# Head norms of a 1-core transformer kernel: squares as two rounded parts, two fp32r products of ones in place of one fp32 product

## The reference

```python
def rms_norm(x, w):
    xf = x.astype(jnp.float32)
    y = xf * lax.rsqrt(jnp.mean(xf * xf, axis=-1, keepdims=True) + EPS)
    return (y * w.astype(jnp.float32)).astype(x.dtype)

# hgrn2_mixer, o: (B, S, heads, 128)
o = rms_norm(o, gate_norm_w) * jax.nn.silu(g...)
return o.reshape(B, S, D_MODEL) @ w_out
# diff_attn_mixer, o: (B, S, heads, 128)
o = rms_norm(o, subln_w) * (1.0 - lam_init)
return o.reshape(B, S, D_MODEL) @ w_out
```

## Time and profile before

| | us |
|---|---|
| median of 3 runs | 2556.8 (2556.59 to 2557.85) |
| the profiled execution's own time | 2557.45 |
| its span in the trace | 2554.4 |
| PE busy | 2499.1 (98% of the span) |
| DVE busy | 1471.3 (58%) |
| ACT busy | 1166.2 (46%) |
| POOL busy | 162.2 (6%) |

### The profile page before, as it was taken

The page is one execution under the profiler, slowest core; times in us unless marked ns, Lnnn a source line. Parts: engine busy times, 40 slices in busy tenths (PEclk is TensorE's granted clock), DMA queues, the critical chain, the costliest instruction groups (busy, mean ns, idle before and its releaser), DMA issues.

```text
span 2554.4 us, 34537 instructions
## 1 busy us (share of the span) xinstructions
PE 2499.1 (98%) x13736; PEld 2033.0 (80%) x13736; DVE 1471.3 (58%) x2374; ACT 1166.2 (46%) x2099; POOL 162.2 (6%) x156
## 2 busy tenths in 40 slices
PE   9999999999999999999989999999999999999998
PEld 6888778888776688888867888888877877788886
DVE  6665554433756565344378888786666556543343
ACT  5454352322456644233256666665455444432232
POOL 2110110000200020000101111111000010100001
PEclk9999999999999999999999999999999999999999
DMA  4222134534322223323232222222321233233322
GB/s 153 76 61 73 58 101 120 127 104 120 98 82 73 66 83 99 99 91 99 91 94 72 67 64 69 73 76 75 95 65 60 93 122 100 76 105 99 95 95 74
DMA packets 197088, 226.41 MB, mean 89 GB/s; under 512 B 7553, under 2 KB 132769, under 8 KB 196673
## 3 DMA queue, kind: packets, MB, share of 16 engines
q1 hardware_dynamic: 196928, 224.21, 29.6%
HBM read 214.22 MB, written 9.44 MB: 88 GB/s over the span
## 4 chain that ended last, share of the span: by engine, by line
PE 83%; DVE 9%; ACT 5%; issue 2%; DMA 0%; POOL 0%; DVEq 0%; SPq 0%; ACTq 0%; POOLq 0%
PE bank L1978 23%; PE bank L1980 22%; PE bank L1979 22%; PE bank L1984 2%; PE bank L1986 2%; PE bank L1985 2%; DVE CV L2710 1%; DVE wlo L2474 1%; PE bank L1997 1%; PE bank L2185 1%; PE bank L2161 1%; ACT whi L2253 1%; DVE h L2508 1%; PE bank L2193 1%; ACT XAh L2262 1%
## 5 line engine op out<-in xcount | busy, mean ns | idle before, releaser
L2474 DVE TENSOR_TENSOR wlo<-raw,whi 128x1024 fp32r<-128x1024 f32 x389 | 489.3, 1264 | 632.5 <-ACT whi L2253 630.3
L2253 ACT ACTIVATE whi<-raw 128x1024 fp32r<-128x1024 f32 x389 | 408.7, 1058 | 587.8 <-PE bank L1980 575.2
L1978 PE MATMUL bank<-XAh,whi 128*128 128x512 f32 x1552 | 616.4, 397 | 12.1 <-issue 5.2
L1980 PE MATMUL bank<-XAh,wlo 128*128 128x512 f32 x1552 | 602.6, 388 | 0.0
L1979 PE MATMUL bank<-XAl,whi 128*128 128x512 f32 x1552 | 602.5, 388 | 0.0
L1978 PEld LDWEIGHTS bank<-XAh,whi 128*128 128x128 f32 x1552 | 292.1, 188 | 91.2 <-issue 23.9
L1980 PEld LDWEIGHTS bank<-XAh,wlo 128*128 128x128 f32 x1552 | 292.1, 188 | 61.3
L1979 PEld LDWEIGHTS bank<-XAl,whi 128*128 128x128 f32 x1552 | 292.4, 188 | 57.5 <-issue 1.0
L1978 PE MATMUL bank<-XBh,whi 128*128 128x512 f32 (+1 forms) x840 | 331.2, 394 | 1.8 <-DVE XBl L2480 1.7
L1980 PE MATMUL bank<-XBh,wlo 128*128 128x512 f32 (+1 forms) x840 | 324.0, 386 | 0.0
L1979 PE MATMUL bank<-XBl,whi 128*128 128x512 f32 (+1 forms) x840 | 323.9, 386 | 0.0
(11 more groups left out here) (346 smaller groups left out, 3329.9 us busy)
## 6 DMA issues: line engine op xcount, KB each, us to landing
raw<-in_w_in SPq DMA_DIRECT2D x77, 512.0 KB, 3.8
raw<-in_up SPq DMA_DIRECT2D x64, 512.0 KB, 3.6
raw<-in_down SPq DMA_DIRECT2D x64, 512.0 KB, 3.7
raw<-in_a_w_in SPq DMA_DIRECT2D x32, 512.0 KB, 4.1
raw<-in_w_up SPq DMA_DIRECT2D x32, 512.0 KB, 3.7
raw<-in_w_down SPq DMA_DIRECT2D x32, 512.0 KB, 3.4
raw<-in_w_kv SPq DMA_DIRECT2D x16, 512.0 KB, 3.6
raw<-in_w_ssd_branch SPq DMA_DIRECT2D x16, 512.0 KB, 3.5
```

Source lines behind the costliest of these rows:

```text
L1978: pe.matmul(out, wh[:, w, c], xh[:, x, r], start=st, stop=False)
L1980: m = pe.matmul(out, wl[:, w, c], xh[:, x, r], start=False, stop=en)
L2253: act.activation(s.hi, s.raw, ACT.Copy).then_inc(s.whi[0], 1)
L2474: dve.tensor_tensor(s.lo, s.raw, s.hi.bitcast(F32), ALU.subtract).then_inc(s.wlo[0], 1)
```

## The change

For the 8 heads of the first mixer and the 8 of the attention, the step `sq` becomes `sq_parts`: ACT squares the bank in fp32 (`sq`), then squares it again with fp32r output (`sqp`, part 0); DVE subtracts part 0 from `sq` and writes the rest as fp32r (`sqp`, part 1). The step `ones` becomes `ones_parts`: two fp32r products of a rounded matrix of ones, one per part, into the same bank. The product waits for the subtraction. There is one buffer `sqp` in each stage; a head's generator waits for it (`his.room(1)`), where attention's heads had two buffers `sq` to wait for. The setup rounds the ones once on ACT and its semaphores are regrouped; `lwork` moves into the first stage's memory.

```diff
+    def square_parts(src, ready, his):
+        q, hi = sqs.take(), his.take()
+        e = add("sq_parts", src=src, src_ready=ready, q=q, hi=hi, sq=sig("sq"), hi_done=sig("sq"), lo_done=sig("sq.lo"))
+        q.free(e.lo_done)
+        return hi, e.lo_done
+
+    def parts_sum(hi, ready, bank):
+        s = add("ones_parts", hi=hi, ready=ready, bank=bank, ones=sig("ones"))
+        hi.free(s.ones)
+        return s.ones
...
-            sq, sqt = square(ob.t[:, :], s7.val)
+            while not his.room(1):
+                yield WAIT
+            hi, lo = square_parts(ob.t[:, :], s7.val, his)
...
-            s8 = add("ones", q=sq, sq=sqt, bank=b, n=S, first=True, final=True, ones=sig("ones"))
-            sq.free(s8.ones)
-            r, rt = rms_close(b, s8.ones, P)
+            r, rt = rms_close(b, parts_sum(hi, lo, b), P)
...
-            while not ring_all.room(2) or not sqs.room(1):
+            while not ring_all.room(2) or not sqs.room(1) or not his.room(1):
                 yield WAIT
...
+        elif k == "ones_parts":
+            on.wait_ge(*K.onesr_ready)
+            on.wait_ge(*s.ready)
+            on.room(s.bank)
+            pe.matmul(s.bank.t[:, :], K.onesr[:, :], s.hi.t[:, 0, :], start=True, stop=False)
+            pe.matmul(s.bank.t[:, :], K.onesr[:, :], s.hi.t[:, 1, :], start=False, stop=True).then_inc(s.ones[0], 1)
...
+        elif k == "sq_parts":
+            on.wait_ge(*s.src_ready)
+            on.room(s.q)
+            act.activation(s.q.t[:, :], s.src, ACT.Square).then_inc(s.sq[0], 1)
+            on.room(s.hi)
+            act.activation(s.hi.t[:, 0, :], s.src, ACT.Square).then_inc(s.hi_done[0], 1)
...
+            act.activation(K.onesr[:, :], K.ones, ACT.Copy).then_inc(s.onesr[0], 1)
...
+        elif k == "sq_parts":
+            on.wait_ge(*s.sq)
+            on.wait_ge(*s.hi_done)
+            dve.tensor_tensor(s.hi.t[:, 1, :], s.q.t[:, :], s.hi.t[:, 0, :].bitcast(F32), ALU.subtract).then_inc(s.lo_done[0], 1)
```

More of the change, by code:

```diff
@@ L304, in make_plan @@
     rrs = Ring([Slot(sb(f"rr{i}", [P, S])) for i in range(2)])
-    K.epst, K.lwork, K.ls2 = sb("epst", [P, 1]), sb("lwork", [P, 128]), sb("ls2", [P, 4])
+    K.onesr = sb("onesr", [P, P], F32R)
+    K.epst, K.ls2 = sb("epst", [P, 1]), sb("ls2", [P, 4])
     K.ident, K.U, K.L, K.ones = (cst[:, c:c + 128] for c in (C_IDENT, C_U, C_L, C_ONES))
@@ L701, in make_plan @@
         over, ring_h = {}, ring_all
+        his = Ring([Slot(sb("sqp", [P, 2, S], F32R, scope=sc))])
+        K.lwork = sb("lwork", [P, 128], scope=sc)
         SCt = Ring([Slot(sb(f"SCt{i}", [P, S], scope=sc)) for i in range(4)])
@@ L878, in make_plan @@
             if k == 5:
-                s = add("setup", lam=sig("lam"), lb=sig("lb"), eps=sig("eps"), lam1=sig("lam1"), lam2=sig("lam2"), lb1=sig("lb1"), lb2=sig("lb2"))
-                K.lam, K.lb, K.eps = s.lam, s.lb, s.eps
+                s = add("setup", eps=sig("setup.dve"), lam1=sig("setup.dve"), lb1=sig("setup.dve"), lam=sig("setup.dve"), lb=sig("setup.dve"),
+                        lam2=sig("setup.act"), onesr=sig("setup.act"), lb2=sig("setup.act"))
+                K.lam, K.lb, K.eps, K.onesr_ready = s.lam, s.lb, s.eps, s.onesr
             split(XB, k, hsrc(k), ht[k], scale=col(gain["a_norm_pre"] + k), src2=K.gain_in)
@@ L1217, in values @@
             hs[hd]["at"].free(s1.val)
-            q, sq = square(ob.t[:, :], s1.val)
+            hi, lo = square_parts(ob.t[:, :], s1.val, his)
             yield
@@ L1223, in values @@
             b = ring_all.take()
-            s3 = add("ones", q=q, sq=sq, bank=b, n=S, first=True, final=True, ones=sig("ones"))
-            q.free(s3.ones)
+            ones_done = parts_sum(hi, lo, b)
             add("act_table", name="natural_log_exp_and_others")
-            r, rt = rms_close(b, s3.ones, P)
+            r, rt = rms_close(b, ones_done, P)
             yield
```

## The result

The changed kernel takes 2561.98 us, the median of 19 runs (2560.45 to 2566.7); the kernel before, run beside it, 2556.95 (19 runs, 2555.97 to 2558.19). The ratio is 1.002, with a 95% interval of 1.0013 to 1.0027: 5.0 us slower. The forecast was 1.5 slower, so the loss is 3.5 us larger than forecast, and that needs an explanation. The time itself is 3.7 us above the stated 2558.3, at the very edge of the range.

A forecast was written before the change was run, and what follows sets the result against it. PE, busy 98% of the span, was taken to bound the kernel. First mixer -2.0, attention heads 0 to 3 +4.8, heads 4 to 7 -1.3 make +1.5 on the median 2556.8: 2558.3 us, range 2553.0 to 2562.0.

The forecast's parts named there:

- The freed 0.41 us a head, first mixer -2.0: First mixer: shorter products free 0.41 us at each of seven heads, last head 0.85 later; -2.0 in all.
- rival C: First mixer: DVE's shift reaches PE there too, four of seven heads lose; +5.6 beyond the forecast, 2563.9; chance 12%.
- Attention, heads 0 to 3, +4.8: Reciprocals wait in DVE's list behind the subtraction, PE starts later: 1.4 + 1.0 + 1.4 + 1.0 = +4.8 us.
- rival B: Middle heads of the attention: the waits are absorbed, -4.9 us in all, 2551.9; chance 13%.
- Attention, heads 4 to 7, -1.3: Four shorter products gain 1.6 and a vanished wait 0.6, head 4's wait costs 1.0; walked through in order -1.3 us.
- Head 4's wait: Attention head 4: PE reaches the product of ones before the subtraction is done and waits 1.0 us.
- the wait of 0.58 for rr: Attention, at 878.90: PE's wait for a bank that rr frees goes, as head 5's product leaves its way.
- From there the subtractions are ready before PE comes: Attention, after head 4: each value product has a whole piece, 2.7 us, behind it, so PE finds subtractions done.
- Rival D, the clock: Mixer's last head and later stages: one clock fall comes or goes, about 1.7 us either way, 2556.6 or 2560.0; chance 15%.
- the 3.2 of the prediction: Last head of the first mixer: PE idles 3.2 us in place of 2.35.
- its own +1.4 at head 0: Attention head 0: ACT's L2327 starts 1.4 us late behind the held reciprocals, and PE starts 1.4 later.
- Rival E: Products of ones get less short than taken, 0.24 us freed a head: +2 on 12 heads, 2560.3; chance 5%.

The follow-up runs named there:

- the half by itself: Changed kernel with the attention's eight heads back to one square and one fp32 product, new form in the first mixer only: 2554.87 us, before 2556.85.
- the three kernels above: Changed kernel, attention's heads with one square and no DVE operation: 2553.69 us; two squares, no DVE operation: 2555.63; one square and a DVE addition: 2557.92.
- the first four experiments: Changed kernel with new form in first mixer only, 2554.87 us; attention only, 2565.02; attention head 5 back to fp32, 2561.05; attention's subtractions on POOL, 2563.08.
- x4_later2: Changed kernel with the attention's second square and subtraction one round later, products of ones a round after that: 2565.11 us, before 2557.34.

## Why the prediction was off

- **The freed 0.41 us a head, first mixer -2.0:** right. 0.4 at each of seven heads, PE's wait at the last one 1.97 (1.95 forecast), and the half by itself measured -2.0. None of PE's waits is new in heads 0 to 6 (0.68 and 0.96 us before and after), so rival C is out.
- **Attention, heads 0 to 3, +4.8:** right in mechanism, and nearly in size: 4.4 in two traces. The split into second square and subtraction is shown by the three kernels above, and rival B (the waits are absorbed) is out. The queue order held: the reciprocals didn't pass the subtraction.
- **Attention, heads 4 to 7, -1.3:** this step failed. Head 4's wait (0.87, forecast 1.0) was right, and the wait of 0.58 for rr went. Wrong was "From there the subtractions are ready before PE comes": they were, but head 7's product waits 1.91 us for a bank instead. I had followed only what the product reads and not where it writes. The tail lost 0.7 where 1.3 were to be gained, which puts the sum 2.0 us off. The same 1.91 without any subtraction shows that the bank and the order make this wait. With the order of before back, the wait is 0.87 and the trace's loss in the tail is gone; the median gives 0.9 us back.
- **Rival D, the clock:** the other half. I gave one fall of 1.7 us 15%, at either sign, and placed it at the mixer's last head. It came there too, and cost nothing, because PE waited behind it anyway. (PE idles 1.97 + 1.65 = 3.6 us at that head without a fall, not the 3.2 of the prediction, which left out that the shorter product makes the wait longer.) Two more came, behind the waits that the change itself made or made longer, and cost 3.2 us in the profiled execution. The forecast left them out of its sum; one of them stood behind the wait that its own +1.4 at head 0 made longer.
- **Sum by the trace:** -2.2 + 4.4 + 0.7 + 3.2 - 0.4 = +5.7, against a span 5.6 longer. The median's loss is 3.5 above the forecast's. By the traces 2.0 of that is the tail; the rest I put down to the clock, but that is argued and not shown. A hint are the granted clocks of all timed runs: 0.9955 on average over the 19 of the changed kernel, 0.9970 over the 28 of before beside the first four experiments. A fall of 3.4 us takes 0.0007 of a run's average, so that is about two falls more in each run, an estimate, at most 1.7 us each. The -0.4 behind the attention I did not trace to a cause.
- Rival E, products less short, is out: 0.23 apart.

## What to carry to other kernels

When PE's wait behind a place names ACT or DVE, an operation put into their lists there is paid almost in full (0.43 us of a second square's 0.50), however low their busy shares: at such a place the idle time of each is the time in which it waits for the other. Where no such wait stands behind, as at heads 0 to 6 of the first mixer, the same operations cost nothing. For every product that such a change moves, follow the bank it writes as well as the tile that it reads. And add to a forecast wait of PE of the size that was followed by falls here (1.70 to 2.60 us) the chance of a clock fall behind it, on the side of the loss.

## What the runs showed of the hardware that I had not expected

**Falls behind short waits.** In six profiles PE waited 1.70 us at attention head 0. In five of them the granted clock then fell to the 1.2 GHz level for some 3.4 us, at 1.6 us of PE's time in the changed kernel; in the sixth, the kernel with heads 0 to 3 alone, it stayed at the full level:

```profile
750.00:760.00 10.00, 7.96 (x41) 5.72 (x40) 7.41 (x24) 6.22 (x15) 0.00 (x0) 1.00 0.36 103
```

In the same stretch of the changed kernel it was 0.83. The other seven profiles, the kernel before among them, have 0.64 to 1.48 us there and no fall. At head 2 the same six, and `x4_later2`, waited 1.70, and none fell. Behind the 1.91 of the tail the clock fell in the changed kernel and in that with the attention alone, and not in two others (two squares without the subtraction, heads 4 to 7 alone). Waits of 2.29 (POOL, head 7), 1.96 and 2.60 us (`x4_later2`, tail) were each followed by a fall, and the 1.97 of the mixer's last head in four of the ten profiles that have it. So a wait of this size was often followed by a fall and not always; that the wait causes it is not shown. The 19 runs of the changed kernel spread over 6.3 us (3.7 without the longest one), those of the kernel before over 2.2, and over up to 3.8 beside the experiments. What decides which executions get a fall was not tested.

**POOL beside DVE.** A POOL subtraction of 1.30 us made the DVE operation that started within it 1.05 long in place of 0.49, and 1.19 in place of 0.35.
